# One tile and one transpose for two complementary blocks of probabilities in a sliding-window mixer, with the bias made by ScalarE

## What is computed

```python
def sliding_window_attention(q, k, v, sinks):
    # q: (B,S,Hkv,G,dh): 16 query heads of 64, 2 key heads; blocks of 128 queries
    rel = QBLK + a_idx - j_idx                  # own and previous block of keys: 256 columns
    alibi = -slopes[:, :, None, None] * rel.astype(jnp.float32)
    def block(args):
        valid = (rel >= 0) & (rel < C_WINDOW) & (key_pos >= 0)    # C_WINDOW = 128
        bias = jnp.where(valid, alibi, MASK_VALUE)
        s = jnp.einsum('bqhgd,bkhd->bhgqk', qi, kb) * scale + bias
        m = jnp.maximum(jnp.max(s, axis=-1, keepdims=True), sink)
        p = jnp.exp(s - m)
        denom = jnp.sum(p, axis=-1, keepdims=True) + jnp.exp(sink - m)
        return jnp.einsum('bhgqk,bkhd->bqhgd', p / denom, vb)
```

## Time and profile before

| | |
|---|---|
| median of 3 runs | 1875.62 us (1875.28 to 1875.63) |
| profiled execution, device time | 1875.19 us |
| its span | 1873.4 us |
| TensorE busy | 1863.8 us, 99% |
| VectorE busy | 1189.3 us, 63% |
| ScalarE busy | 794.5 us, 42% |
| granted TensorE clock | 1.0 of full speed |

### The profile page before, as it was taken

One profiled execution on the slowest core, in us unless ns is written; L12 is line 12 of the kernel. 1 busy time (PEld: TensorE's weight loads), 2 busy tenths in 40 slices (PEclk: granted clock), 3 DMA queues, 4 the chain that ended last, 5 costly groups with the idle time before them and its releaser, 6 DMA issues.

```text
span 1873.4 us, 24493 instructions
## 1 busy us (share of the span) xinstructions
PE 1863.8 (99%) x9034; PEld 1500.0 (80%) x9034; DVE 1189.3 (63%) x1846; ACT 794.5 (42%) x1198; POOL 143.5 (8%) x105
## 2 busy tenths in 40 slices
PE   9999999999999999999999999999999999999999
PEld 7767888888887788888888887888777788888887
DVE  6686676356646866763566498675666667643762
ACT  5365443133436754431334343422577544322441
POOL 1022000000021020000000101121211010000000
PEclk9999999999999999999999999999999999999999
DMA  6212222322231122223222322435433122223223
GB/s 219 83 53 68 90 90 90 112 91 92 82 106 58 64 72 90 95 85 112 93 101 80 119 90 93 146 127 187 131 130 113 68 90 90 81 98 112 90 79 101
DMA packets 39521, 185.99 MB, mean 99 GB/s; under 512 B 4448, under 2 KB 5856, under 8 KB 24848
## 3 DMA queue, kind: packets, MB, share of 16 engines
q1 hardware_dynamic: 39152, 184.77, 29.1%
q10 hardware_dynamic: 288, 0.16, 0.0%
HBM read 176.42 MB, written 8.49 MB: 99 GB/s over the span
## 4 chain that ended last, share of the span: by engine, by line
PE 94%; DVE 4%; ACT 1%; issue 0%; DMA 0%; SPq 0%; DVEq 0%; ACTq 0%
PE banks L760 55%; PE banks L1298 22%; PE banks L807 5%; PE banks L837 1%; PE banks L1212 1%; PE banks L1237 1%; PE banks L1223 1%; PE banks L1346 1%; DVE w_lo L1999 1%; PE banks L1375 1%; DVE tmp L2385 1%; PE banks L1358 1%; PE banks L1311 1%; ACT w_hi L1452 1%; PE banks L969 1%
## 5 line engine op out<-in xcount | busy, mean ns | idle before, releaser
L760 PE MATMUL banks<-xn_hi,w_hi 128*128 128x512 f32 x1208 | 468.3, 391 | 0.0
L760 PE MATMUL banks<-xn_hi,w_lo 128*128 128x512 f32 x1208 | 466.1, 389 | 0.0
L760 PE MATMUL banks<-xn_lo,w_hi 128*128 128x512 f32 x1208 | 466.1, 389 | 0.0
L1452 ACT ACTIVATE w_hi<-raw 128x2048 fp32r<-128x2048 f32 (+2 forms) x134 | 228.3, 1703 | 227.9 <-PE banks L760 190.0
L1999 DVE TENSOR_TENSOR w_lo<-raw,w_hi 128x2048 fp32r<-128x2048 f32 (+2 forms) x134 | 273.6, 2042 | 48.5 <-ACT w_hi L1452 48.0
L760 PEld LDWEIGHTS banks<-xn_hi,w_hi 128*128 128x128 f32 x1208 | 226.7, 188 | 48.9 <-issue 1.2
L760 PEld LDWEIGHTS banks<-xn_lo,w_hi 128*128 128x128 f32 x1208 | 226.7, 188 | 48.4 <-issue 1.2
L760 PEld LDWEIGHTS banks<-xn_hi,w_lo 128*128 128x128 f32 x1208 | 226.7, 188 | 46.8
L1514 ACT ACTIVATE tmp<-scaled_h,par 128x512 f32<-128x512 f32 x132 | 100.7, 809 | 349.9 <-DVE scaled_h L2049 349.8
L2049 DVE TENSOR_TENSOR scaled_h<-banks,token_rs 128x512 f32<-128x512 f32 x132 | 85.1, 687 | 185.9 <-PE banks L760 165.6
L1298 PE MATMUL banks<-xn_hi,w_hi 128*128 128x512 f32 x400 | 161.2, 403 | 0.6 <-DVE big L2099 0.6
(11 more groups left out here) (290 smaller groups left out, 2632.8 us busy)
## 6 DMA issues: line engine op xcount, KB each, us to landing
raw<-weights SPq DMA_DIRECT2D x114, 1024.0 KB, 4.9
raw<-weights SPq DMA_DIRECT2D x24, 768.0 KB, 4.4
raw<-weights SPq DMA_DIRECT2D x24, 640.0 KB, 3.9
big<-scratch SPq DMA_DIRECT2D x40, 256.0 KB, 4.5
att<-scratch SPq DMA_DIRECT2D x16, 256.0 KB, 4.0
scratch<-stage SPq DMA_DIRECT2D x12, 256.0 KB, 4.6
scratch<-con SPq DMA_DIRECT2D x12, 256.0 KB, 2.2
raw<-weights SPq DMA_DIRECT2D x4, 512.0 KB, 3.6
```

What stands on the lines that cost most here:

```text
L760: return pe.matmul(psum[:, 2 * p + m, :], w[:, at_:at_ + P], x_part(k), start=start, stop=stop)
L1452: act.activation(w_hi[:, sl], raw[:, sl], ACT.Identity).then_inc(hi_done, 1)
```

## The change

The two 128-column halves of a row of scores are merged after the maxima: where one block is masked its negated score is very large, so the minimum of the two halves is the visible one (`tensor_tensor` with `min`, a pack). A row then has 128 columns instead of 256 in the exponential, in `finish`, in the transpose and in the copy. After the transpose the tile is 256 columns for both blocks. The sum over both key blocks is written as P V_prev + (P masked to the own block) (V_own - V_prev): a new `masked` multiplies the transposed tile by a triangle, and `v_diff`, made once, holds the differences of the values. The number of value matmuls is the same. In the first query block the masked tile is not needed. The bias of a pair is formed by ScalarE instead of VectorE. Semaphores of the three mixers' split squares are merged into two (`head_high`, `head_rest`); `c_pack`, `c_masked` and `c_biased` are new, and the order of the squares is unchanged.

```diff
+        v_diff = chunk(att, 3)
+        def c_packs(r, m, b):
+            return 6 * (r // 2) + (m + 1 if r % 2 == 0 else 2 + 2 * m + b + 1)
 # TensorE, turn and values
-                        for b, i, w in c_blocks(r):
-                            for j in range(256 - w, 256, P):
-                                last = pe.transpose(psum[:, 6 + m, 256 * b + j:256 * b + j + P], c_prob(m, r, b)[:, j:j + P], ident)
+                        for b in range(2):
+                            last = pe.transpose(psum[:, 6 + m, b * P:(b + 1) * P], c_prob(m, r, b)[:, P:2 * P], ident)
...
-                            pe.wait_ge(c_v, 1)
+                            pe.wait_ge(c_v, 2)
...
                     pe.wait_ge(c_copied, 2 * r + 2)
+                    pe.wait_ge(c_masked, 2 * r + 2)
                     for b, i, w in c_blocks(r):
-                        first = max(i - 1, 0)
-                        for j in range(first, i + 1):
+                        parts = [(vtok[0], max(i - 1, 0), b * P)] + ([(v_diff, i - 1, (2 + b) * P)] if i else [])
+                        for n, (v, j, from_) in enumerate(parts):
 # ScalarE, exps, copy, bias
-                            act.wait_ge(c_max, n)
-                            pr = c_prob(m, r, b)[:, 256 - w:257]
+                            if i:
+                                act.wait_ge(c_pack, c_packs(r, m, b))
+                            else:
+                                act.wait_ge(c_max, 4 * r + 2 * m + 1)
+                            pr = c_prob(m, r, b)[:, P:2 * P + 1]
...
-                        act.activation(c_slot(m, r)[:, c0:T], psum[:, 6 + m, c0:T], ACT.Identity).then_inc(c_copied, 1)
+                        act.activation(c_slot(m, r)[:, 0:2 * P], psum[:, 6 + m, 0:2 * P], ACT.Identity).then_inc(c_copied, 1)
+                def alibi(it, m):
+                    if it >= 2:
+                        act.wait_ge(c_max, 8 * (it - 1))
+                    act.activation(c_bias[it % 2][:, 256 * m:256 * m + 256], ccol("window", 0, 256), ACT.Identity,
+                                   scale=ccol("c_slope", 2 * it + m)).then_inc(c_biased, 1)
...
                     if 1 <= r <= C_ROUNDS:
                         copy(r - 1)
+                    if r // 2 + 1 < C_PAIRS:
+                        alibi(r // 2 + 1, r % 2)
 # VectorE
                     if r % 2 == 0:
                         me.wait()
+                        dve.wait_ge(c_biased, 2 * it + 2)
...
+                    for m in range(2):
+                        dve.wait_ge(c_max, 4 * r + 2 * m + 2)
+                        for b, i, w in c_blocks(r):
+                            if i:
+                                pr = c_prob(m, r, b)
+                                dve.tensor_tensor(pr[:, P:2 * P], pr[:, 0:P], pr[:, P:2 * P], ALU.min).then_inc(c_pack, 1)
...
-                            pr = c_prob(m, r, b)[:, 256 - w:256]
+                            pr = c_prob(m, r, b)[:, P:2 * P]
                             last = dve.tensor_scalar(pr, pr, row_inv[:, 2 * i + m:2 * i + m + 1], None, ALU.mult)
...
+                def masked(r):
+                    b0 = 1 - r % 2
+                    for m in range(2):
+                        dve.wait_ge(c_copied, 2 * r + m + 1)
+                        dve.tensor_tensor(c_slot(m, r)[:, (2 + b0) * P:T].rearrange("p (j l) -> p j l", j=2 - b0),
+                                          c_slot(m, r)[:, b0 * P:2 * P].rearrange("p (j l) -> p j l", j=2 - b0),
+                                          ccol("tri", 0, P).rearrange("p (o l) -> p o l", o=1).to_broadcast([P, 2 - b0, P]), ALU.mult).then_inc(c_masked, 1)
...
-                alibi(0, 0)
-                alibi(0, 1)
...
+                dve.wait_ge(c_v, 1)
+                dve.tensor_tensor(v_diff[:, 0:3 * P], vtok[0][:, P:T], vtok[0][:, 0:3 * P], ALU.subtract).then_inc(c_v, 1)
...
-                    if r // 2 + 1 < C_PAIRS:
-                        alibi(r // 2 + 1, r % 2)
...
+                    if 1 <= r <= C_ROUNDS:
+                        masked(r - 1)
```

More of the change, by code:

```diff
@@ L235, in blocks_program @@
         A_SPLIT, C_SPLIT, X_SPLIT = (4, 5), (3, 5, 6, 8), tuple(range(4, 16))
+        C_PARTS = len(A_SPLIT)
+        X_PARTS = C_PARTS + len(C_SPLIT)
         sub_rs = chunk(more, 0)
@@ L295, in blocks_program @@
         c_turned_v, c_v = sem("c_turned_v"), sem("c_v")
+        c_pack, c_masked, c_biased = sem("c_pack"), sem("c_masked"), sem("c_biased")
         c_scored, c_max, c_exp, c_fin = sem("c_scored"), sem("c_max"), sem("c_exp"), sem("c_fin")
@@ L675, in _ @@
                             pool.wait_ge(d_sq, n + 1)
-                            pool.wait_ge(d_high, A_SPLIT.index(n) + 1)
-                            pool.tensor_tensor(sq_rest[which], (sq_q, sq_k)[which], sq_high[which].bitcast(F32), ALU.subtract).then_inc(d_rest, 1)
+                            pool.wait_ge(head_high, A_SPLIT.index(n) + 1)
+                            pool.tensor_tensor(sq_rest[which], (sq_q, sq_k)[which], sq_high[which].bitcast(F32), ALU.subtract).then_inc(head_rest, 1)
                     for h in range(A_HEADS - 1):
@@ L1179, in x_norm_job @@
                 if n in X_SPLIT:
[L1180 removed]
+                    pe.wait_ge(head_rest, X_PARTS + X_SPLIT.index(n) + 1)
                     split_stat(1, n).then_inc(f_stat, 1)
@@ L1368, in values @@
                     pe.wait_ge(c_copied, 2 * r + 2)
+                    pe.wait_ge(c_masked, 2 * r + 2)
                     for b, i, w in c_blocks(r):
-                        first = max(i - 1, 0)
-                        for j in range(first, i + 1):
+                        parts = [(vtok[0], max(i - 1, 0), b * P)] + ([(v_diff, i - 1, (2 + b) * P)] if i else [])
+                        for n, (v, j, from_) in enumerate(parts):
                             for m in range(2):
                                 at_ = j * P + 64 * m
-                                from_ = 256 * b + 256 - w + (j - first) * P
-                                last = pe.matmul(psum[64 * m:64 * m + 64, 2, i * P:(i + 1) * P], vtok[0][:, at_:at_ + 64],
+                                last = pe.matmul(psum[64 * m:64 * m + 64, 2, i * P:(i + 1) * P], v[:, at_:at_ + 64],
                                                  c_slot(m, r)[:, from_:from_ + P],
-                                                 start=(i == 0), stop=(i == 3 and j == 3), skip_group_check=True)
+                                                 start=(i == 0), stop=(i == 3 and n == 1), skip_group_check=True)
                     last.then_inc(c_pv, 1)
@@ L1566, in square_high @@
                         act.wait_ge(d_stat, n - 1)
-                    act.activation(sq_high[which], chunk(big, 4 * which + it), ACT.Square).then_inc(d_high, 1)
+                    act.activation(sq_high[which], chunk(big, 4 * which + it), ACT.Square).then_inc(head_high, 1)
                 def pooled_high(c):
@@ L1716, in c_stage @@
                 act.activation(vtok[0], psum[:, 2, :], ACT.Identity).then_inc(c_v, 1)
+                alibi(0, 0)
+                alibi(0, 1)
                 norm_job(1)
@@ L1886, in square_high @@
                         act.wait_ge(f_stat, n - 1)
-                    act.activation(sq_high[which], f_qkv[it % 2][which], ACT.Square).then_inc(f_high, 1)
+                    act.activation(sq_high[which], f_qkv[it % 2][which], ACT.Square).then_inc(head_high, 1)
                 def exps(r):
```

23 lines of the change are left out of this document (8 added, 15 removed).

## The result

| | before | after |
|---|---|---|
| median | 1875.62 us (1875.20 to 1875.89) | 1885.32 us (1884.93 to 1886.14) |
| ratio | | 1.0053, interval 1.0041 to 1.0064 |
| span of the profiled execution | 1873.4 us | 1883.5 us |

The change costs 9.7 us; 7.4 were forecast. The page shows TensorE busy for less time than before in a span that is longer.

What follows compares the result with a forecast made beforehand. TensorE bounds the kernel before; after it, the VectorE-ScalarE chain leads: +7.2 us over the loop and 0.2 of tail, +7.4 us (TensorE stalls 12.4, transposes save 5.0), giving 1883.0 us, range 1873 to 1890.

Steps and rivals of the forecast that it cites:

- the chain from maxima to maxima: VectorE and ScalarE, second mixer's loop: order of dependent steps, not summed work, sets the pace; 93.1 us over rounds 0 to 14.
- 48 transposes off: TensorE turns fall from 6 or 8 transposes to 4; at 0.105 us each, 5.0 us off.
- the two gates named: TensorE's even-round values wait for `output` (1.15 us slack left), even-round scores for `scaled` (1.0 us left).
- The wait of the filling in round 10: TensorE's filling waits for round 9's low weight half; the chain is later still, so it adds nothing.
- A turn of four transposes: Sign in TensorE's next profile: a transposed turn is 0.44 us long instead of 0.65 to 0.87.
- Short operations: VectorE operations of 128 columns last 0.29 us but occupy 0.21 through overlap; VectorE's net work rises 12.4 us.
- Rounds with weights: Rounds 1, 5, 9 and 11, where weights are split, take 8.3, 7.45, 7.5 and 8.3 us and stall TensorE.
- Plain rounds: Chain of 5.75 us (odd) and 5.05 (even), 10.8 a pair; forecast wrong if rounds 3, 7, 13 are under 5.5.
- masks of 256 columns: VectorE's wide masks last 0.42 us and occupy 0.34 us each, 16 of them in the loop.
- worse: Rival, chance 0.10: short operations occupy their whole length, squares run beside packs and masks, clock may fall: 1887 to 1893 us.
- The saving stands: Rival, chance 0.10: the chain stays inside TensorE's rounds and the 48 transposes come off: 1870.6 us.
- it cancels: Rival, chance 0.20: chain 0.3 to 0.5 us a round shorter than forecast, 1876 to 1879 us, or 1873.

Runs made afterwards that it cites:

- e4: Changed kernel with ScalarE's half-slab high-weight conversions moved from behind copies and bias to the head of the round: 1876.27 us, ratio 1.0003.
- e3: Changed kernel with the bias of a pair moved back from ScalarE to VectorE, ahead of `evacuate`: 1884.08 us, ratio 1.0045.
- e2: Changed kernel with each head's packs issued right behind that head's maxima instead of behind all four: 1885.52 us, ratio 1.0053.
- e5: Changed kernel with the edits of e1 and e4 together: 1873.41 us, ratio 0.9987.
- e9: e5 with the edit of e7 added: 1872.57 us, ratio 0.9984.
- e10: e9 with VectorE forming `output` before the next round's maxima in every even round from 4 on: 1872.07 us, ratio 0.9981.
- e6: Kernel before the change with only ScalarE's half-slab conversions moved to the head of the round: 1875.43 us, ratio 1.0000.
- e7: Changed kernel with GpSimd's squares of rounds 2 and 8 waiting for that round's finish: 1883.38 us, ratio 1.0045.
- e8: Changed kernel with six needless TensorE matmuls ahead of the scores of rounds 4 and 12, and the wait for maxima moved ahead of them: 1884.87 us, ratio 1.0051.
- e1: Changed kernel with VectorE's masks of a round moved behind the finish of the next round: 1883.14 us, ratio 1.0039.

## Why the prediction was right, and what was mis-sized

- **Which engine leads.** Right: the chain from maxima to maxima through VectorE and ScalarE sets the loop. e4 takes away a wait, with all work the same, and gives back 9.0 us; e3 adds 3.5 us of VectorE work and the time does not grow. But e2 and e3 also show that in rounds 2, 6, 9 and 12 the chain is VectorE's own queue without a gap, where each added operation counts.
- **TensorE.** 48 transposes off, 5.0 us forecast; TensorE's busy time in e4, e5, e9 and e10, where few stalls are left, is 1858.2 to 1858.5 us against 1863.8 before (1862.5 in e6, which has the same transposes, so the saving is known to about 1 us). Its idle time in the loop is 10.6 us, inside the forecast 10 to 15, two thirds of it at the two gates named. The wait of the filling in round 10, which was to add nothing, is 1.3 us. A turn of four transposes is 0.60 to 0.83 us long in the timeline, not 0.44; the 0.65 and 0.87 given with it for six and eight were likewise under the 0.82 and 1.03 of the earlier trace rows.
- **Short operations.** Right: four packs last 0.89 us together and one 0.29, so they are 0.20 us apart (0.21 forecast). VectorE's busy time rose by 10.1 us on the page and 10.5 in like windows (12.4 forecast, 11 to 13 as the sign to look for), a little less than forecast: the finishes had lost time beside the squares before, and the masks lose it now. The bias on ScalarE was put a little low: it lasts 499 ns, with 0.40 us from its start to that of the conversion behind it (587.97 to 588.37), where 0.35 was taken.
- **Rounds with weights.** Right to 0.16 us: 8.25, 7.29, 7.36 and 8.25 for 8.3, 7.45, 7.5 and 8.3. The text listed these rounds as what hides nothing, and e4 shows that rounds 1, 5 and 11 with round 0 are most of the loss. That they "cannot be brought under 7 us" holds for this order only: in e4 rounds 1, 5 and 11 take 5.84, 5.57 and 6.43 us with the same work.
- **Plain rounds.** The odd ones measured 5.57 (5.75 forecast), above the 5.5 under which the forecast would have been wrong; with the 5.16 of round 2 without its square (e7) a plain pair makes 10.7 us, where 10.8 was forecast. The masks' wait for the copies in plain rounds was there, 0.72 us in rounds 3 and 7.
- **The mis-sized term** is the masks of 256 columns, costed at 0.34 us apiece. In rounds 2, 4, 6 and 8 one of each pair stood beside a square of GpSimd. The pairs of these rounds took 2.7 us more than 0.75 each, and the steps came out 2.95 us long, more than the whole miss of the chain (8.8 measured, 7.0 forecast); the other steps being short by 1.15 leaves 1.8. In round 4 the square explains 0.23 of the 0.73 us: there ScalarE's copies waited 0.44 us for transposes that came late behind TensorE's stall of 1.62 us and the slow filling. That 7.4 came so near 9.7 is in part luck, since the short steps cover more than a third of the long ones. The squares were named only in the rival "worse". They could have been priced: the trace of before has this row for `finish`, whose first operation stood there then.

```profile
L2304 DVE TENSOR_SCALAR att<-att,small 128x128 f32<-128x128 f32 x16 | 7.9, 497 | 0.3
```

  Its 128 columns have a mean of 497 ns against 348 for the 256 columns in the same list. The timelines say why: the four multiplications of round 8 stood beside a square, those of round 12 did not.

```profile
625.15 1.04 POOL L695 TENSOR_TENSOR tn<-big 128x512 f32<-128x512 f32 x1 [9.06 <-DVE big L2255]
```

```profile
625.19 1.80 DVE L2304 TENSOR_SCALAR att<-att,small 128x128 f32<-128x128 f32 x4
...
652.19 1.01 DVE L2304 TENSOR_SCALAR att<-att,small 128x128 f32<-128x128 f32 x4
```

  The five rounds with a square have 1.58 to 1.81 us, 3.4 us too long together, about what the masks lose in the changed kernel (2.9 in five rounds). It cost nothing then, when VectorE waited for TensorE anyway, and it costs in full when VectorE leads.
- **The rest.** The span grew by 10.1 us: 8.6 between the first and the last scores, 0.5 behind them (0.2 forecast) and 1.0 ahead of them. The last is no steady effect of the change: the first scores started between 576.1 and 577.4 us in all these profiles, at 576.12 in e7 and 576.36 in e8, which do the same ahead of them.
- **The rivals.** "The saving stands" and "it cancels" both fail with the changed kernel. Once the order is mended the times come near theirs, e4 to 1876.3 and e10 to 1.5 us from the 1870.6 of the saving; that is no proof of the mechanism given for the cancelling, a chain shorter by 0.3 to 0.5 us in every round, for e4 shortens three long rounds and one other. "Worse" had both its causes right and their price too high: the squares lie beside the masks (2.9 us) and the clock does fall (0.5 us at most), but short operations do overlap.

## What to carry to other kernels

When two engines are level, follow the dependency from one round's operation to the same one of the next round and add it up with every instruction queued in front; a moved wait costs what stands behind it, and here moving the one conversion that was queued behind new waits gave back 9.0 of the 9.7 us. Do it round by round: here some rounds were set by the loop through two engines and others by VectorE's queue alone, and an edit that helped the first (e2) cost as much in the second. A lesson of e6: the same reordering is worth nothing before the change, so judge an order by the kernel in which it has to work. Look in the list by shape for a narrow form that is slower than a wide one, and in the timelines for what runs beside it: here it was a contention that was free until that engine led.

## What the runs showed of the hardware

- Two-input VectorE operations of 256 columns in SBUF that met a running GpSimd `tensor_tensor` of 512 columns ended 0.61 to 0.62 us behind its end in all five rounds, whether that made 0.94 or 1.60 us for the pair instead of 0.75: they waited, rather than ran slower side by side. Beside the masks alone (rounds 4, 8 and 10) the GpSimd operation kept its 1.04 us. It took 1.95 in round 2, where a VectorE split of 1024 columns (L2262, 594.56 to 595.78) had begun before it, and that kept its 1.22: the one that came second lost. The maxima, which read PSUM and SBUF, kept their 0.48 us beside the same square (e7). When the finish stood there instead (e5), it took the loss: four operations lasted 1.64 us instead of 0.87.

```profile
625.87 1.64 DVE L2326 TENSOR_SCALAR att<-att,small 128x128 f32<-128x128 f32 x4
```

- An operation that waits for the maxima straight before it on VectorE starts 0.12 us later than an independent one (e2).
- The granted clock fell to 0.50 behind a gap of 1.62 us on TensorE, between rounds with further waits, and stayed there for about 3 us; in e8, with the gap filled, it stayed at 1.00. The Trainium skill (TensorE: Matmul & The Clock Gate, section "HAM oscillation — how this bites in real kernels") warns that gaps bring the half clock back, and the trace agrees for this gap. The length of one gap does not tell it, though: behind 1.65 us at the values of round 12 in the same trace, and behind 1.25 and twice 1.65 us in e7, the clock stayed at 1.00. Off the critical path its cost was under what could be measured; in e1, where VectorE then waited for scores, it was up to 0.9 us.
